# Two-block transformer on one core: rotary halves exchanged by transfers inside SBUF instead of a matrix product

## The reference, cut to what matters

```python
def apply_rope(x, cos, sin):
    half = x.shape[-1] // 2
    x1, x2 = x[..., :half], x[..., half:]
    return jnp.concatenate([x1 * c - x2 * s, x2 * c + x1 * s], axis=-1)

def diff_attention(hn, w_qkv, w_o, ...):
    q, k, v = jnp.split(hn @ w_qkv, ...)
    q = apply_rope(q.reshape(B, S, 2 * H, d), cos, sin)
    k = apply_rope(k.reshape(B, S, 2 * H, d), cos, sin)
    # per head: softmax of q0 k0 minus lam times softmax of q1 k1, times v, then an rms norm
    return o.reshape(B, S, DIFF_V_WIDTH) @ w_o
```

## Time and profile before

| what | value |
|---|---|
| median of 3 runs | 1133.8 us (1133.43 to 1134.47) |
| the profiled execution | 1133.16 us, span 1131.8 us |
| granted TensorE clock | 0.999 of full speed |
| PE busy | 1118.6 us, 99% of the span |
| DVE busy | 822.1 us, 73% |
| ACT busy | 637.6 us, 56% |
| chain of work that ended last | PE 85%, DVE 6%, ACT 5%, DMA 2% |

### The profile page before, as it was taken

How to read it: one execution, slowest core, us unless ns; L and a number is a source line. 1 busy time by engine, 2 the same in 40 slices (tenths; PEclk the granted TensorE clock), 3 DMA queues, 4 the chain that set the end, 5 groups by cost and what they waited for, 6 DMA issues and landing times.

```text
span 1131.8 us, 16844 instructions
## 1 busy us (share of the span) xinstructions
PE 1118.6 (99%) x6542; PEld 980.0 (87%) x6542; DVE 822.1 (73%) x1417; ACT 637.6 (56%) x1202; POOL 53.8 (5%) x68
## 2 busy tenths in 40 slices
PE   9999999999999999999999999999999999999997
PEld 7998999799988888888899988888889988888886
DVE  6998878798666766676777867666667866766665
ACT  6664444856757755555755556444556654555553
POOL 2100000000001000000012300000001100000000
PEclk9999999999999999999999999999999999999999
DMA  9989999684232666668453336555554434655530
GB/s 385 420 324 377 331 353 264 226 343 155 104 113 75 244 211 222 220 223 206 146 188 112 117 108 224 187 188 186 190 182 166 166 113 152 209 191 189 192 127 37
DMA packets 36992, 231.10 MB, mean 204 GB/s; under 512 B 6825, under 2 KB 8241, under 8 KB 9522
## 3 DMA queue, kind: packets, MB, share of 16 engines
q1 hardware_dynamic: 31536, 225.59, 56.5%
q10 hardware_dynamic: 5378, 4.45, 1.3%
HBM read 228.95 MB, written 1.07 MB: 203 GB/s over the span
## 4 chain that ended last, share of the span: by engine, by line
PE 85%; DVE 6%; ACT 5%; DMA 2%; issue 1%; POOL 1%; ACTq 0%; DVEq 0%; POOLq 0%; SPq 0%
PE pacc L1724 42%; PE ps L1724 42%; DVE wlo L2274 2%; ACT whi L2002 1%; DMA raw<-in_stream 1%; ACT arena L2109 1%; DMA cl<-in_cols 1%; ACT wk L2212 1%; POOL st L2610 1%; DVE raw L2294 1%; DVE st L2505 0%; PE ps L1861 0%; DVE wk L2499 0%; DVE wlo L2284 0%; PE ps L1932 0%
## 5 line engine op out<-in xcount | busy, mean ns | idle before, releaser
L2274 DVE TENSOR_TENSOR wlo<-raw,whi 128x1024 fp32r<-128x1024 f32 x346 | 414.9, 1223 | 115.8 <-ACT whi L2002 115.4
L1724 PE MATMUL ps<-both,whi 128*128 128x256 f32 (+2 forms) x1728 | 457.0, 339 | 1.1 <-DVE both L2371 0.6
L2002 ACT ACTIVATE whi<-raw 128x1024 fp32r<-128x1024 f32 x346 | 360.5, 1057 | 96.8 <-PE ps L1724 45.3
L1724 PE MATMUL ps<-both,wlo 128*128 128x256 f32 x1264 | 348.6, 281 | 0.0
L1724 PEld LDWEIGHTS ps<-both,whi 128*128 128x128 f32 (+1 forms) x1728 | 294.5, 189 | 41.6 <-issue 2.3
L1724 PEld LDWEIGHTS ps<-both,wlo 128*128 128x128 f32 x1264 | 236.2, 189 | 2.9
L1724 PE MATMUL pacc<-whi,both 128*128 128x512 f32 (+2 forms) x352 | 106.4, 383 | 1.0 <-ACT both L2125 0.6
L2002 ACT ACTIVATE sg<-ps 128x256 f32<-128x256 f32 (+1 forms) x98 | 37.3, 380 | 100.0 <-PE ps L1724 99.8
L1724 PE MATMUL pacc<-whi,mhi 128*128 128x512 f32 x228 | 90.7, 398 | 0.0
L2294 DVE SCALAR_TENSOR_TENSOR raw<-raw,silu_c 128x1024 f32<-128x1024 f32 x72 | 89.3, 1249 | 1.3 <-DMA raw<-in_stream 1.3
L1724 PE MATMUL pacc<-whi,mlo 128*128 128x512 f32 x228 | 89.4, 392 | 0.0
(11 more groups left out here) (280 smaller groups left out, 1470.5 us busy)
## 6 DMA issues: line engine op xcount, KB each, us to landing
raw<-in_stream SPq DMA_DIRECT2D x213, 1024.0 KB, 5.1
gates<-gate_rows ACTq DMA_DIRECT2D x3, 512.0 KB, 7.6
h<-in_x SPq DMA_DIRECT2D x2, 512.0 KB, 4.3
cst<-in_const ACTq DMA_DIRECT2D x1, 1024.0 KB, 4.7
arena<-bias_rows ACTq DMA_DIRECT2D x1, 1024.0 KB, 20.0
arena<-in_final_g SPq DMA_DIRECT2D x1, 512.0 KB, 5.9
out<-tmp SPq DMA_DIRECT2D x2, 256.0 KB, 2.0
out<-tmp ACTq DMA_DIRECT2D x2, 256.0 KB, 2.3
```

What stands on the lines that cost most here:

```text
L1724: return e.matmul(o, a, b, start=start, stop=stop)
L2002: return e.activation(o, a, ACT.Copy, **how)
L2274: return e.tensor_tensor(o, a, hi.bitcast(F32), ALU.subtract)
```

## The change

For fifteen of the sixteen blocks (all but the last k block) `swapped` takes the place of `roped`. ACT copies the block into one of three new places in SBUF, and the PSUM bank is given back right after that copy. SP then issues four transfers from SBUF to SBUF, 32 rows of 1 KB each, which exchange the halves of the block. POOL multiplies by the cosine as before. A new step `rope_close` on DVE waits for the transfers, multiplies by the sine and adds. No PE work is left in the rotation. The minus sign moves from the matrix `rot` into the sine table.

`rope_close` of block i comes after the nudge that follows block i+1 and before the split that `feed()` emits there. In DVE's order block i now has: the heads' work after block i, the sums of block i-1, the low part of the weight unit. Both kernels set `rest[0]` to 2; a block now counts as rotated one nudge later than before.

In the loop over the sixteen blocks the chunk loads are issued by ACT and not by SP: `feed()` only notes that a load is owed, and `load_owed()` emits it in the next block, after ACT's copy of that block and before the nudge. ACT waits there for the low part of the unit split one block before. The places, order and number of everything else in the stage stay.

```diff
+    owed, loader = [], ["sp"]
     def load_chunk():
+        if loader[0] == "act":
+            owed.append(0)
+        else:
+            load_next()
+    def load_owed():
+        while owed:
+            owed.pop()
+            load_next()
+    def load_next():
         n = pos["chunk"]
...
-        add("load", chunk=n, free=latest(*free))
+        add("load", chunk=n, free=latest(*free), lane=loader[0])
...
+    slots, swaps = Places([Place(n) for n in range(3)]), Counter()
+    def swapped(dst, split, b, tk, s, by):
+        slot = slots.take()
+        n, (at, t_tables) = slot.at, by
+        x, y = tick("rpc"), tick("rpz")
+        swaps[n] += 64
+        add("rope_swap", b=b.at, full=tk, s=s, n=n, free=slot.free, at=at, tables=t_tables, copied=x)
+        banks.give(b, x)
+        yield
+        sine = tick("rps")
+        add("rope_close", n=n, cosine=y, swapped=(f"swap{n}", swaps[n]), sine=sine, at=at, dst=dst, split=split)
+        t = tick("rpd", 2 if split else 1)
+        slots.give(slot, t)
+        yield t
...
+    pending, rest[0], loader[0] = [], 2, "act"
     for hh in range(8):
         for g in (0, 8):
...
-            rope = roped(("kT", hh) if g else ("qT", hh), not g, b, tk, 1.0 if g else 0.125, by_r)
+            last = g and hh == 7
+            rope = (roped if last else swapped)(("kT", hh) if g else ("qT", hh), not g, b, tk, 1.0 if g else 0.125, by_r)
             next(rope)
+            load_owed()
             side.nudge()
+            if pending:
+                at, was = pending.pop()
+                t_q[at], born[at] = next(was), side.now
             feed()
-            side.soon(rope_end(g + hh, rope))
+            if last:
+                side.soon(rope_end(g + hh, rope))
+            else:
+                pending.append((g + hh, rope))
+    load_owed()
+    loader[0] = "sp"
...
+        elif st.kind == "rope_swap":                      # SP
+            q.wait_ge(*st.copied)
+            x, s, _ = m.swap_slot(st.n)
+            for a in range(0, P, 32):
+                c = a ^ 32
+                e.dma_start(s[a:a + 32, :], x[c:c + 32, :]).then_inc(S[f"swap{st.n}"], 16)
...
+        elif kind == "load" and st.lane == "act":         # ACT
+            q.room(st.free)
+            n = st.chunk % NR
+            e.dma_start(m.raw[:, n, :], d["stream"][st.chunk]).then_inc(S[f"raw{n}"], 16)
...
+        elif kind == "rope_close":                        # DVE
+            what, h = st.dst
+            _, s, y = m.swap_slot(st.n)
+            q.wait_ge(*st.swapped)
+            q.wait_ge(*st.cosine)
+            o = s if st.split else m.kT[:, h, :]
+            e.tensor_tensor(o, s, m.rope_table(st.at, "sin"), ALU.mult).then_inc(S["rps"], 1)
+            q.wait_ge(*st.sine)
+            if st.split:
+                for c, r in enumerate(LOHI):
+                    e.tensor_tensor(m.qT[r, 2 * h + c, :], s[r, :], y[r, :], ALU.add).then_inc(S["rpd"], 1)
+            else:
+                e.tensor_tensor(o, o, y, ALU.add).then_inc(S["rpd"], 1)
```

More of the change, by code:

```diff
@@ L1358, in schedule @@
             tk = block(b, 0, unit(("qk", g + hh)), n1, side.nudge)
-            rope = roped(("kT", hh) if g else ("qT", hh), not g, b, tk, 1.0 if g else 0.125, by_r)
+            last = g and hh == 7
+            rope = (roped if last else swapped)(("kT", hh) if g else ("qT", hh), not g, b, tk, 1.0 if g else 0.125, by_r)
             next(rope)
+            load_owed()
             side.nudge()
+            if pending:
+                at, was = pending.pop()
+                t_q[at], born[at] = next(was), side.now
             feed()
-            side.soon(rope_end(g + hh, rope))
+            if last:
[4 more added lines that the diff above has]
+    loader[0] = "sp"
+    rest[0] = 2
     while banks.leaving:
@@ L1546 @@
     "xsq", "xg", "xnew", "xrow", "xz", "xzd", "xah", "xhi", "xlo", "phi", "plo", "fin", "wa", "wb",
-    "ixc", "ixt", "mod", "g8", "masks", "tabc",
+    "rpc", "rpz", "swap0", "swap1", "swap2", "ixc", "ixt", "mod", "g8", "masks", "tabc",
     "lows", "sums", "sg", "hm", "hhi", "hlo", "rsilu", "rgate",
@@ L1628, in __init__, with swap_slot @@
         self.fg = self.arena[:, 6144:7168]
+    def swap_slot(self, n):
+        x, y = self.view(4096, 8, T), self.view(11776, 3, T)
+        return x[:, n, :], x[:, 3 + n, :], y[:, n, :]
     def view(self, at, n, width):
@@ L1700, in sync_program @@
     for st in steps:
-        if st.kind == "load":
+        if st.kind == "load" and st.lane == "sp":
             q.room(st.free)
@@ L2241, in scalar_program @@
             copy(m.sg[:, st.x, :], m.bank(st.b)[:, 0:T], scale=st.s).then_inc(S["rpx"], 1)
+        elif kind == "rope_swap":
+            q.wait_ge(*st.full)
+            q.room(st.free)
+            copy(m.swap_slot(st.n)[0], m.bank(st.b)[:, 0:T], scale=st.s).then_inc(S["rpc"], 1)
         elif kind == "lambda":
@@ L2632, in gpsimd_program @@
             e.tensor_tensor(m.hm[:, st.y, :], m.sg[:, st.x, :], m.rope_table(st.at, "cos"), ALU.mult).then_inc(S["rpy"], 1)
+        elif kind == "rope_swap":
+            q.wait_ge(*st.copied)
+            q.wait_ge(*st.tables)
+            x, _, y = m.swap_slot(st.n)
+            e.tensor_tensor(y, x, m.rope_table(st.at, "cos"), ALU.mult).then_inc(S["rpz"], 1)
 def build(nc, stream, x, c_row, cols, const, rel, lam, final_g, out):
@@ L2660, in constants @@
     for m in range(P):
[L2661 to L2664, removed]
+        r[m + 32 if m % 64 < 32 else m - 32, m] = 1.0
     put("rot", r)
@@ L2673, in constants @@
     put("cos", np.cos(ang).astype(np.float32).T[i % 32])
-    put("sin", np.sin(ang).astype(np.float32).T[i % 32])
+    put("sin", np.sin(ang).astype(np.float32).T[i % 32] * np.where(i % 64 < 32, -1.0, 1.0)[:, None].astype(np.float32))
     t = np.arange(T)
```

## The result

The changed kernel takes 1145.29 us (median of 5, 1144.01 to 1146.37) against 1133.43 us of the kernel before on the same chip: the ratio is 1.0102, 95% interval 1.0087 to 1.0116, slower by 11.9 us. I had 1138.5 us: the direction was right, the size less than half. The profiled execution took 1145.12 us, span 1143.3.

A forecast was written before the change was run, and what follows sets the result against it. DVE, as full as PE, was taken to bound the stage: -0.8 + 5.5 + 0.65 + 0.4 = +5.75 us, with 0.4 us of room +5.35, so 1133.16 became 1138.5 us; range 1131.0 to 1140.5.

The forecast's parts named there:

- ACT's moved load: Loads waiting on ACT delay head work on DVE: +5.5 us over five even blocks, +0.65 after block 4, +0.4 after block 15.
- DVE as the bound: Q/k stage: DVE takes 9.98 us a pair of blocks against PE's 9.45, leaving 0.4 us of room at head 7.
- (a): Rival: DVE bounds the stage but ACT's wait costs nothing, pairs stay 9.98 us; 1132.0 us, chance 0.20.
- (b): Rival: PE bounds to the end and all 6.7 us are kept, DVE pairs at 8.6 us; 1126.5 us, chance 0.09.
- (c): Rival: transfers land late and DVE waits for them mid-stage too, +1 to +3 us, 1140 to 1141.5 us; chance 0.07.
- the turns of heads 3, 4, 5 and 7: Sign: PE idle at L1932 of these heads, waiting for DVE's mix, 2 to 3 us each.
- +1.1 us: DVE's L2301 delayed by ACT's late high part and squares after blocks 6, 8, 10, 12 and 14, +1.1 us each.
- I take no change: DVE's sine product reading SBUF instead of PSUM: no change in length, 0.1 us either way for each of 15.
- 0.4 us are then lost: Block 0: DVE waits 0.4 us for the transfers at an assumed 2.5 us, up to 3 us at the upper bound.
- the 1.6 us that I had credited there: Head 0's maxima on DVE: start 1.6 us earlier because PE has three rotations and a 0.29 us wait less.
- forecast 12: PE's idle time: its 6.7 us saved plus 5.35 us more return as waits, 12 us in all.
- My +5.35 us: Delay of PE's turn of head 7 and all behind it: DVE's mix +5.75 us, with 0.4 us of room.

The follow-up runs named there:

- experiment 1: Kernel before with PE's permutation product of fifteen rotations left out, DVE multiplying the unrotated half (output differs): 1131.52 us, ratio 0.9979 to the kernel before.
- experiment 8: Kernel of experiment 3 with the rotation's sums put inside the heads' waits on DVE: 1128.49 us, ratio 0.9951 to the kernel before; again 1128.19 us, 0.9957.
- experiment 9: Kernel before, PE's product kept, with the rotation's sums one block later and inside the heads' waits: 1132.20 us, ratio 0.9998 to the kernel before.
- experiment 4: Changed kernel, loads still on ACT, with the rotation's sums ahead of the heads' work on DVE: 1141.87 us, ratio 1.0077 to the kernel before.
- experiment 5: Changed kernel with the loads still on ACT but behind the heads' work of the same block: 1140.53 us, ratio 1.0067 to the kernel before.
- experiment 10: Changed kernel with only the rotation's sums moved inside the heads' waits, loads still on ACT: 1135.25 us, ratio 1.0024 to the kernel before.
- experiment 3: Changed kernel with the chunk loads back on SP, at the same places of the list: 1136.76 us, ratio 1.0024 to the kernel before.
- experiment 6: Kernel of experiment 3 with POOL's cosine product narrowed from 256 to 8 columns (output differs): 1134.20 us, ratio 0.9999 to the kernel before.
- experiment 7: Kernel of experiment 3 with blocks 0 and 1 rotated by PE's product as before: 1136.12 us, ratio 1.0019 to the kernel before.

## Why the prediction was right in its way and wrong in its size

In short: that DVE's list bounds the stage and that ACT's moved loads lengthen it was right. The sum was too small, because the sums of the rotation were put at no change, the transfers at block 0 at 0.4 us, and PE's return at the full clock.

**DVE as the bound: right.** DVE's list with its chain waits was read from rows 5 to 7 as the second bound, and experiments 1, 8 and 9 show it from three sides: PE relieved alone gives 2.4 us, DVE relieved alone nothing, both together about 5 us.

**The order of the rivals: right.** (a) and (b) needed DVE's pairs at 10 or 8.6 us; they were 11.9. (c), late transfers in the middle of the stage, didn't happen in the changed kernel, where DVE waited for a transfer once, at block 0. Its mechanism is real, though: single transfers took up to 5.7 us to land here, and DVE waited for them in the middle or at the end of the stage in experiments 4, 5 and 10. "It needs DVE to do a pair in 8.6 us, so it would have to be freed of most of its waits" was what experiment 8 then did.

**PE's waits: the wrong instruction.** I had PE waiting at the turns of heads 3, 4, 5 and 7. It waited at the products of q and k, for the k block's sums (11.3 us in six waits, and 1.0 us more for block 15's), because the sums stand behind the head's work of the next block. I had only asked who waits for the mix. By experiment 4 it made no difference to what bounds.

**ACT's moved load: mechanism right, its step right.** "+1.1 us" was 1.1 to 1.2. At block 8 the split that starts at 615.77 holds DVE for 1.14 us, to 616.91; L2360 starts at 618.49, 1.58 us later, where the earlier trace rows have 0.39. After block 4 it was 0.7 us (0.65), after block 15 0.3 (0.4), in all 0.2 us more than forecast. (The first load, after block 2, I had left out; DVE's wait there, 0.72 us, was 0.95 before.) But experiment 3 took away 8.8 us, not 6.7. With the loads gone the sums of k blocks hardly met POOL any more and those of q blocks did so oftener (next point), net 0.8 us, and DVE no longer waited for PE, 1.0 us.

**"I take no change" for the sums: wrong, +2.8 us.** This is the step that failed most. A k block's sums took 1.15 us instead of 0.89 at five places, a q block's 1.8 to 1.9 instead of 1.35 at four of seven, 3.3 us together. The sums of before had themselves met POOL a little (1.68 us at 606.56, 1.44 at two others), 0.5 us over the 1.35, so the change is 2.8 us. I had compared only the two lengths, and not asked what POOL does meanwhile. In the changed kernel ACT's copy of an odd block stands behind the load, so POOL's cosine product starts when DVE comes to the sums:
```profile
631.70 0.73 POOL L2709 TENSOR_TENSOR arena<-arena 128x256 f32<-128x256 f32 x1 [0.33 <-ACT arena L2053]
```
and the sine product beside it, with both inputs in SBUF, takes 0.78 us. The product that reads PSUM never took more than 0.42 us in this stage of the kernel before, with POOL at work beside it too (at 612.91, in POOL's product of 612.03 to 613.60). Experiment 6 shows the cause. The Trainium skill ("VectorE: DVE Perf Modes", section "Two Vector instructions with no wait between them") says that an instruction with two SBUF inputs reads the second one through an interface shared with GpSimd; the trace agrees, 0.78 against 0.42 us. Weighed before, that rule would have given a term with a sign.

**The transfers at block 0: "0.4 us are then lost": wrong, 1.7.**
```profile
584.11 0.42 DVE L2609 TENSOR_TENSOR arena<-arena 128x256 f32<-128x256 f32 x1 [1.69 <-DMA arena<-arena]
```
I had taken 2.5 us for all four together. Each lands in 2 us, but SP issues them one after another, 0.6 us each with 0.04 between: the last starts at 582.14 and lands at 584.1, 3.9 us after ACT's copy ended at 580.2. So head 0's maxima came at 589.79 as before (589.80), and the 1.6 us that I had credited there didn't come. That the transfers took them is read from the chain; experiment 7 removed this wait and the time didn't follow.

**DVE's waits for PE: not foreseen, +1.0 us.** With PE late behind the sums and its clock at 0.50 in the 3 us after, DVE waited 0.66 us twice for the second product of a head. From the maxima to the end of the mix it was 4.0 us there instead of 3.5, so each wait cost 0.5. I had let PE come back from every wait at full speed. For the same 6512 records it was busy 1113.0 us in experiment 1 and 1117.3 here, so 4.3 of the 6.45 us that the rotations gave were lost again on PE. PE was idle for 12.7 us of the stretch from 576 to 676 us; that I had forecast 12 is luck, since both its terms were off.

My +5.35 us with these terms (1.6 + 2.8 + 1.0 + 0.2) is 10.95; measured are 11.3 at head 7's turn. The last 0.4 us I can't assign.

## What to carry to other kernels

Before work is taken from the busiest engine, read the waits of the second one: if it never waits for the first, it is a bound too, however low its busy share, and its waits inside a dependent chain count as its length. Such waits are where work can be put: the same instructions moved between the maxima and the mix turned a loss of 0.2% (experiment 3) into a gain of 0.45%. The gain needs both halves: the same filling gave nothing while PE kept its product. A DMA issue moved to a computing engine costs what its wait holds back, here 7 to 9 us for eight issues of 0.34 us.

## What the runs showed of the hardware

In the changed kernel four transfers of 32 KB inside SBUF behind one wait cost 0.6 us each to issue on SP and 1.8 to 5.7 us each to land (median 2.4); at block 0 that made 3.9 us from the data being ready to DVE starting. Started just behind the issue of a 1 MB load by ACT, the last one took 4.5 and 4.9 us (experiments 4 and 5). A DVE product of two SBUF operands, 128 x 256, took 0.78 us in the changed kernel and up to 0.97 us in the others (experiment 8, at 639.02) where 0.41 is its least, while POOL worked in SBUF; with one operand in PSUM it stayed at 0.42 in the kernel before. PE's granted clock fell to 0.50, 1.2 GHz, for about 3 us each from 610 and from 634 us, behind waits of PE of 3.56 and 3.10 us.
